# Latent attention's gate as seven block products a pair, with weight sums on GpSimd

## The reference

```
def _mla_layer(x, w_in, q_norm, w_uq, w_out, k_nope, k_rope, v):
    hproj = x @ w_in
    q_lat, gate = hproj[..., :Q_LORA], hproj[..., Q_LORA:]
    q = (_rms_norm(q_lat, q_norm) @ w_uq).reshape(b, s, H_B, QK_NOPE + QK_ROPE)
    ...
    o = _causal_block_attention(q_nope, q_rope, k_nope, k_rope, v).reshape(b, s, WIDTH_B)
    return (o * jax.nn.silu(gate)) @ w_out
```

## Time and profile before

| | |
|---|---|
| median of 3 runs | 1378.1 us (1377.26 to 1378.14) |
| profiled execution, its own time | 1378.76 us |
| span of the profile | 1376.7 us |
| PE busy | 1359.8 us, 99% |
| DVE busy | 1010.8 us, 73% |
| ACT busy | 745.6 us, 54% |
| POOL busy | 306.1 us, 22% |

### The profile page before, as it was taken

How to read it: one execution, slowest core, us unless ns; L and a number is a source line. 1 busy time by engine, 2 the same in 40 slices (tenths; PEclk the granted TensorE clock), 3 DMA queues, 4 the chain that set the end, 5 groups by cost and what they waited for, 6 DMA issues and landing times.

```text
span 1376.7 us, 19133 instructions
## 1 busy us (share of the span) xinstructions
PE 1359.8 (99%) x7308; PEld 1174.4 (85%) x7308; DVE 1010.8 (73%) x1671; ACT 745.6 (54%) x1197; POOL 306.1 (22%) x161
## 2 busy tenths in 40 slices
PE   8999999999999999999999999999999999999998
PEld 6788888888888888888888888878888999988887
DVE  7979787889933755454545479946877888889895
ACT  5453535457545534443444356658965666676554
POOL 2051414110043433433344210025304000000000
PEclk9999999999999999999999999999999999999999
DMA  7458575385367988966796558363122576455552
GB/s 269 164 180 225 194 206 186 127 281 206 134 186 216 312 216 238 296 171 167 212 300 161 153 212 305 123 202 124 67 85 77 162 206 169 149 181 214 196 190 103
DMA packets 53898, 260.37 MB, mean 189 GB/s; under 512 B 5568, under 2 KB 10304, under 8 KB 28224
## 3 DMA queue, kind: packets, MB, share of 16 engines
q1 hardware_dynamic: 37152, 163.04, 33.9%
q0 software_dynamic: 5760, 41.95, 15.5%
q10 hardware_dynamic: 10912, 54.40, 11.2%
HBM read 252.03 MB, written 91.23 MB: 249 GB/s over the span
## 4 chain that ended last, share of the span: by engine, by line
PE 82%; DVE 11%; DMA 2%; ACT 2%; issue 1%; POOL 1%; SPq 0%; DVEq 0%; ACTq 0%; POOLq 0%
PE bank L631 22%; PE bank L632 22%; PE bank L633 22%; PE bank L1362 6%; PE bank L1424 3%; PE bank L1313 3%; DVE wlo L2317 2%; PE bank L1341 1%; DMA stage<-in_w 1%; DMA v_spill<-v_tok 1%; DMA cols<-in_cols 1%; DVE wlo_a L2317 1%; DVE ar_lo L2317 1%; DVE xres L2495 1%; PE bank L1504 1%
## 5 line engine op out<-in xcount | busy, mean ns | idle before, releaser
L810 POOL TENSOR_TENSOR wlo<-stage,whi 128x1024 fp32r<-128x1024 f32 (+2 forms) x68 | 169.8, 2529 | 428.8 <-ACT whi L1644 342.5
L1647 ACT ACTIVATE whi<-stage 128x1024 fp32r<-128x1024 f32 (+2 forms) x155 | 148.2, 1002 | 104.2 <-PE bank L633 92.2
L2317 DVE TENSOR_TENSOR wlo<-stage,whi 128x1024 fp32r<-128x1024 f32 (+1 forms) x133 | 152.8, 1178 | 9.8 <-ACT whi L1647 9.8
L631 PE MATMUL bank<-xhi,whi 128*128 128x256 f32 (+1 forms) x300 | 98.4, 328 | 2.2 <-POOL wlo L946 1.2
L632 PE MATMUL bank<-xlo,whi 128*128 128x256 f32 (+1 forms) x300 | 98.1, 327 | 0.0
L633 PE MATMUL bank<-xhi,wlo 128*128 128x256 f32 (+1 forms) x300 | 98.0, 327 | 0.0
L1644 ACT ACTIVATE whi<-stage 128x1024 fp32r<-128x1024 f32 (+2 forms) x74 | 76.1, 1079 | 19.5 <-issue 14.3
L631 PE MATMUL bank<-whi,xhi 128*128 128x512 f32 (+1 forms) x204 | 78.3, 384 | 2.1 <-DVE wlo L2317 1.3
L633 PE MATMUL bank<-whi,xlo 128*128 128x512 f32 (+1 forms) x204 | 77.3, 379 | 0.0
L632 PE MATMUL bank<-wlo,xhi 128*128 128x512 f32 (+1 forms) x204 | 77.2, 378 | 0.0
L631 PEld LDWEIGHTS bank<-xhi,whi 128*128 128x128 f32 x300 | 57.0, 190 | 7.8 <-DVE hid L2527 1.4
(11 more groups left out here) (501 smaller groups left out, 4365.2 us busy)
## 6 DMA issues: line engine op xcount, KB each, us to landing
stage<-in_w SPq DMA_DIRECT2D x71, 1024.0 KB, 4.9
tsum<-in_w ACTq DMA_DIRECT2D x32, 1024.0 KB, 12.8
stage<-tsum SPq DMA_DIRECT2D x32, 1024.0 KB, 4.8
tsum<-in_w POOLq DMA_DIRECT2D x16, 1024.0 KB, 9.9
tsum<-tsum POOLq DMA_DIRECT2D x16, 1024.0 KB, 9.9
stage<-in_w SPq DMA_DIRECT2D x8, 1152.0 KB, 6.3
usum<-in_w POOLq DMA_DIRECT2D x8, 1024.0 KB, 10.0
stage<-usum SPq DMA_DIRECT2D x32, 256.0 KB, 4.1
```

The lines of the kernel that those rows point to most:

```text
L631: pe.matmul(dst, a_hi, b_hi, start=start, stop=False, skip_group_check=onto)
L810: pool.tensor_tensor(lo[:, to], stage[p % 2][:, r], hi[:, to].bitcast(F32), ALU.subtract).then_inc(w_lo, 1)
L1647: act.activation(dst, src, ACT.Copy, scale=scale).then_inc(signal, 1)
L2317: dve.tensor_tensor(dst, src, hi.bitcast(F32), ALU.subtract).then_inc(signal, 1)
```

## The change

The gate of a pair is a product of x (512 x 1024) with 1024 x 256 weights. It is cut into two by two blocks on either side, and is computed with seven block products (a scheme of Strassen and Winograd) where eight are plain. Each product is 12 matmuls of 256 columns (`gate_block`). The sums of x (`x_t1` to `x_t4`) are made once ahead of the loop: VectorE adds into `xsum`, ScalarE rounds, VectorE makes three remainders and GpSimd the fourth in the first pair. They lie in space of `vs_a`, `vs_b` (which is the first half of `xres`) and `xhi`, so `xres` is written out to `x_spill` ahead and read back behind the loop. The products are dealt over the pair: four between the scores of head 0 and its transposes, one after the scores of head 1, two after head 1's transposes.

The sums of the weights are made by GpSimd in the staging buffers (`gate_sum`, four of 512 columns a pair). The gate takes two panels, p+2 and p+3, so that a pair has four; of p+2 only 1536 columns are loaded and of p+3 1024, and 2048 and 1536 are split. Partial results are kept in `gate_kept` and summed by VectorE (`add_up`). The split of the next pair's query panel moves to the exponentials of head 1 (first half) and behind `tanh(0)` (second half). The copies for the last layer's sums are dealt over six pairs, one to three in each.

```
+            def gate_sum(pair, i):
+                p = M0 + 4 * pair + (3 if i == 4 else 2)
+                near, far = (stage[(M0 + k) % 2] for k in (0, 1))
+                to, x, y, op = ((slot(near, G_S1), slot(near, G_S3), slot(near, G_S1), ADD),
+                                (slot(near, G_S2), slot(near, G_S1), slot(near, G_A11), SUB),
+                                (slot(near, G_S3), slot(near, G_A11), slot(near, G_S3), SUB),
+                                (slot(far, G_S4), slot(far, G_A12), slot(near, G_S2), SUB))[i - 1]
+                if i in (1, 4):
+                    pool.wait_ge(landed[p % 2], LANDED[p % 2] + 16 * ((p - B0) // 2 + 1))
+                if i > 1:
+                    pool.wait_ge(m_ws, USED + 4 * pair + (2 if i == 4 else 1))
+                pool.tensor_tensor(to, x, y, op).then_inc(m_ws, 1)
...
+            for k in range(4 * PAIRS):
+                split_lo(M0 + k, PANEL if k % 4 == 0 else PAN)
...
+                if k == 0 or k > 1 and k % 4 == 1:
+                    for i in (1, 2, 3):
+                        gate_sum(k // 4, i)
...
                     scores(0)
-                    for i in range(24):
-                        gate_product(0, i)
+                    pe.wait_ge(t_l, USED + 3)
+                    pe.wait_ge(m_kvlo, c(4, 2))
+                    gate_block(x_t2, p + 2, G_S2, 0, bank[1][:, first_t])
+                    gate_block(x_t3, p + 2, G_S3, 0, bank[1][:, second_t]).then_inc(m_g, 1)
+                    gate_block(x_b11, p + 2, G_A11, 1, bank[0][:, first_t])
+                    gate_block(x_t1, p + 2, G_S1, 1, bank[0][:, second_t], True).then_inc(m_g, 1)
                     pe.wait_ge(m_kvlo, c(4, 4))
+                    pe.wait_ge(m_k, c(1, USED + 1))
                     for i in range(10):
                         turn(0, i)
                     scores(1)
-                    pe.wait_ge(m_gt, c(2, 3))
-                    for i in range(12):
-                        gate_product(1, i)
+                    pe.wait_ge(m_u, c(5, USED + 3))
+                    gate_block(x_b21, p + 3, G_A12, 0, bank[0][:, first_t], True)
                     attend(0, bank[1])
                     for i in range(10):
                         turn(1, i)
-                    for i in range(12, 24):
-                        gate_product(1, i)
+                    gate_block(x_b22, p + 3, G_S4, 0, bank[0][:, second_t], True).then_inc(m_g, 1)
+                    pe.wait_ge(t_l, USED + 4)
+                    gate_block(x_t4, p + 3, G_A22, 1, bank[5][:, first_t]).then_inc(m_g, 1)
                     attend(1, bank[7])
...
             act.wait_ge(n_x, TT)
+            act.dma_start(t["x_spill"], xres[:, 0:3, :]).then_inc(aux["x"], 16)
             act.dma_start(wkr[:, :], t["wkr"]).then_inc(aux["kr"], 16)
             act.dma_start(mask[:, :], t["mask"]).then_inc(aux["kr"], 16)
...
+            act.wait_ge(aux["x"], 32)
+            for i, x in enumerate((x_t3, x_t1, x_t2)):
+                act.wait_ge(t_s, USED + i + 1)
+                copy(x[0], xsum[:, (2, 0, 1)[i]], t_h)
...
                     exps(0)
+                    act.wait_ge(m_g, c(4, 5))
+                    act.wait_ge(m_gt, c(3, 3))
+                    copy(gate_kept[:, 0:SEQ], bank[1][:, :], m_k)
+                    act.wait_ge(m_ws, c(4, USED + 4))
+                    split_hi(p + 3, m_kv, c(4, 4), PAN, n)
...
                     exps(1)
+                    next_hi(0)
                     for b in range(3):
                         turned(1, b)
+                    act.wait_ge(m_u, c(5, USED + 4))
+                    tanh(0, first_t, bank[0][:, first_t])
+                    tanh(0, second_t, gate_kept[:, 0:HALF])
+                    next_hi(1)
                     if last and s == 1:
                         act.wait_ge(bld[0], 32)
                         operand_hi(BO, 0)
-                    tanh(1)
+                    act.wait_ge(m_u, c(5, USED + 5))
+                    tanh(1, slice(0, SEQ), gate_kept[:, HALF:])
...
+            s1, s2, s3, s4 = (xsum[:, i] for i in range(4))
+            own.mark(dve.tensor_tensor(s1, *plain(x_b12), ADD))
+            own.mark(dve.tensor_tensor(s2, *plain(x_b22), ADD))
+            own.settle()
+            dve.tensor_tensor(s3, s2, s1, SUB).then_inc(t_s, 1)
...
+            for i, x in enumerate((x_t3, x_t1, x_t2)):
+                dve.wait_ge(t_h, USED + i + 1)
+                lo_of(x[1], (s3, s1, s2)[i], x[0], t_l)
...
                     softmax(0)
+                    dve.wait_ge(m_k, c(1, USED + 1))
+                    dve.wait_ge(m_g, c(4, 6))
+                    add_up(0)
+                    dve.wait_ge(m_u, c(5, USED + 1))
+                    add_up(1)
+                    dve.wait_ge(m_u, c(5, USED + 2))
+                    add_up(2)
+                    for b in range(3):
+                        turned(0, b)
                     softmax(1)
                     for b in range(3):
                         turned(1, b)
+                    dve.wait_ge(m_g, c(4, 7))
+                    add_up(3)
+                    gates(0, 0, first_t, bank[0][:, first_t])
+                    gates(1, 0, second_t, kept[0])
+                    gated(0, bank[1])
+                    dve.wait_ge(m_g, c(4, 8))
+                    add_up(4)
                     if last and s == 1:
                         operand_lo(BO, 0)
-                    gates(1)
+                    gates(2, 1, slice(0, SEQ), gate_kept[:, HALF:])
                     gated(1, bank[7])
```

More of the change, by code:

```diff
@@ L710, in store @@
                                  gt[:, e, :]).then_inc(m_st[e], 16)
-            for j in range(6):
-                load(M0 + j, PANEL if j % 3 == 0 else PAN)
-            with sp.Fori(1, PAIRS // 2) as i:
-                for s in range(2):
[L716 to L720, removed]
+            load(M0, PANEL)
+            load(M0 + 1)
+            load(M0 + 2, PAN, 0, 512)
+            load(M0 + 3, 1024)
+            load(M0 + 4, PANEL)
+            load(M0 + 5)
+            load(M0 + 6, PAN, 0, 512)
+            with sp.Fori(0, PAIRS // 2 - 1) as i:
+                for s in range(2):
+                    store(2 * i + s)
+                    load(M0 + 4 * s + 7, 1024, 8 * i)
+                    load(M0 + 4 * s + 8, PANEL, 8 * i)
+                    load(M0 + 4 * s + 9, PAN, 8 * i)
+                    load(M0 + 4 * s + 10, PAN, 8 * i, 512)
+            store(PAIRS - 2)
+            load(L0 - 1, 1024)
             sp.wait_ge(w_lo, 2 * (L0 - 1))
             seven_load(BO, 0)
-            store(PAIRS - 2)
+            sp.wait_ge(m_g, 4 * PAIRS + 2)
+            sp.dma_start(xres[:, 0:2, :], t["x_spill"][:, 0:2, :]).then_inc(aux["x"], 16)
             sp.wait_ge(w_lo, 2 * L0)
@@ L1353, in attend, with gate_block @@
                         last.then_inc(m_o, 1)
-                    def gate_product(m, i):
-                        wh, wl = panel(p + 2, KX)
-                        k, f = i // 3, slice(m * P, (m + 1) * P)
-                        if m == 0 and i % 3 == 0:
-                            need(p + 2, n, KX, k)
-                        left, right = ((wh, xhi), (wh, xlo), (wl, xhi))[i % 3]
-                        last = pe.matmul(bank[0][:, :], left[:, k, f], right[:, k, :], start=i == 0, stop=i == 23)
-                        if i == 23:
-                            last.then_inc(m_g, 1)
+                    def gate_block(x, panel_, k, late, dst, onto=False):
+                        wh, wl = [slot(w[:, LINE:], k).rearrange("p (k n) -> p k n", k=PK) for w in parts(panel_)]
+                        pe.wait_ge(w_lo, 2 * n + (2 * panel_ + 1 + late))
+                        for kk in range(PK):
+                            last = split_dots(pe, dst, wh[:, kk, :], wl[:, kk, :], x[0][:, kk, :], x[1][:, kk, :],
+                                              kk == 0 and not onto, kk == PK - 1, onto)
+                        return last
                     pe.wait_ge(b_krlo, 4)
@@ L1636, in _, with split_hi @@
         def _(act):
-            def split_hi(p, used=None, count=0, width=PAN, n=0):
+            def split_hi(p, used=None, count=0, width=PAN, n=0, halves=(0, 1)):
                 act.wait_ge(landed[p % 2], 8 * n + LANDED[p % 2] + 16 * ((p - B0) // 2 + 1))
@@ L1641, in split_hi @@
                     act.wait_ge(used, count)
-                for s in range(2):
+                for s in halves:
                     r, to = half_at(p, s, width)
@@ L3003, in _ @@
             for d in range(2, 13):
+                if d == 8:
+                    dve.wait_ge(aux["x"], 64)
                 gathers(BO, 1, d)
```

151 lines of the change are left out of this document (101 added, 50 removed).

## The result

The changed kernel takes 1410.13 us (median of four runs, 1406.69 to 1418.57) beside 1378.12 of the kernel before on the same chip: ratio 1.0243, 95% interval 1.0197 to 1.0288, 32 us slower. Forecast were 1382 and a range of 1372 to 1390: right in sign, wrong in size. The profiled execution took 1409.27 (span 1407.5).

The account below looks back on a forecast made before the run. TensorE, busy 99% of the span, was taken as the bound, so removed matmul time is removed span. Terms: -8.4 + 4.0 + 2.1 + 0.5 + 2.0 + 0.5 + 3.0 = +3.7 us, forecast 1382, range 1372 to 1390.

Parts of the forecast that it names:

- the term of the sum DMAs: Pairs 2, 3, 6, 7: weight sums queue behind a DMA awaiting an accumulate; 0.5 us in all, bounds 0 and 8.
- rival (c): GpSimd's queue becomes the bound: accumulate landing past 12 us, scores wait 2 us in four pairs; 1390, chance 0.12.
- The gate's matmuls: Each pair's gate: 84 matmuls of 256 columns take 10.0 us against 11.05; gain 8.4 us in all.
- the estimate that the prediction made from the Trainium skill: Gate matmuls: straight line between page spacings gives 98 ns for 256 columns, a loss of 1.9 us a pair.
- Second transposes: Each pair: VectorE's two-SBUF-input sum waits for GpSimd, stalling the second transposes 0.5 us; 4.0 us in all.
- The next query panel: Pair's end: the next query panel's later split stalls TensorE 0.3 us, seven times; 2.1 us in all.
- Ahead of the loop: Before the pairs: x_spill delays loads, sums of x delay B0+4 (2.0 us); pair 0's weight sums hold a norm add (0.5).
- Behind the loop: First output product: operand rounding and remainder come later, TensorE stalls 3.0 us; bounds 1.5 and 3.5.
- rival (a): Whole kernel: the matmuls' gain survives, the loop stalls mostly go; -4 us, 1374, chance 0.21.

Follow-up runs that it names:

- e12: Changed kernel with its order of sum DMAs and weight sums kept, the sixteen copies issued ahead of the pair loop; 1397.75 us.
- m1: Test computing nothing of the reference: eight GpSimd sum DMAs of 1 MB, 512 bytes of descriptor scratch; each issue waited for the landing ahead (10.64, 20.51).
- e5: Changed kernel with the weight sums first and every sum DMA moved, none behind the query panel at a pair's start; 1383.66 us, ratio 1.0043.
- e2: Changed kernel with the three weight sums ahead of the sum DMA that follows split_lo(p+1), nothing else moved; 1396.6 us.
- e8: e6 with the first output product's operand rounded and its remainder taken ahead of the last pair's gate sums and tanh; 1376.15 us.
- e6: e5 with the first output product's eight weight copies dealt over pairs 0 and 1, the other sixteen over pairs 2 to 6; 1373.06 us, ratio 0.9965.
- m2: The same eight sum DMAs as m1 with 2048 bytes of descriptor scratch; seven went out at once, the eighth at the seventh landing (44.27).

## Why the prediction was wrong

- **The step that failed** is the term of the sum DMAs, 0.5 us with bounds 0 and 8, and the price and pairs of rival (c), 1390 at a chance of 0.12. The mechanism was told link by link as it came: accumulate, weight sums, ScalarE, `kn_hi`, scores. Even its threshold, "free up to a landing time of 12 us", stands between the 10.5 of e12 (free) and the 14.6 of pair 3 (1.6 us). Three sizes in it were wrong. The landing was taken from a median, 9.9; beside two or three copies, the stores and the loads of a pair's start it was 14.5 to 16.3, and the single transfers of the old timeline (issued at 544.56, landed at 562.08, beside copies too) would have said so. The pairs were taken to be those where a semaphore asks for the earlier sums; GpSimd stood before a sum DMA in every pair from 1 on, which is what m1 shows for a ring of 512 bytes. And in pair 1 a second sum DMA, ahead of the `split_lo(p+1)` itself, was overlooked: 8.97 us of wait. e5, which has e2's order too, puts 26 us of the 32 on the places of these DMAs and the weight sums, the slow matmuls behind the waits included.
- **The clock** was no term at all. The four waits above add up to 29 us; loop and gains would need some 42 (32.4 of loss and about 10 of gain). The transposes take 2 of the rest and the query product 1. Some 9 are matmuls at the lower clock behind five of the waits: in pair 1 the keys' product takes 8.23 us for 5.44, and in pairs 0, 2, 4 and 5 one scores block takes 4.54 to 4.62 for some 3.0.
- **The gate's matmuls**, -8.4: right way, too small, and past its bound of 9.3. Seven blocks take 9.65 us a pair in e5_respread (12 matmuls in 1.36 to 1.38, 0.114 each) where 10.0 was forecast: 1.4 gained a pair, -11.2 in all. The V product, the nearest row, still takes its 0.1177 each in the changed kernels; the gate's spacing is another. With the longer query product (0.07) and second transposes (0.26) taken off, such a pair is 46.21 - 45.15 = 1.06 shorter. The rows also stay apart from the estimate that the prediction made from the Trainium skill, "TensorE: Matmul & The Clock Gate", section Back-to-back issue gap: there 256 columns cost three quarters of 512 (98 and 131 ns), here half (114 and 227).
- **Second transposes**, 4.0: mechanism right (the sum took 1.12 where 1.0 was forecast, R to the second transposes 7.30), size 0.27 a pair, 2.2 in all. It shows as longer transposes, not as a listed wait.
- **The next query panel**, 2.1: no wait on `wlo` in pairs 2 to 7; the query product takes 12.35 to 12.47 for 12.30, at most 1.
- **Ahead of the loop**, 2.0 + 0.5: +0.65. `wkr` did queue behind the store (it landed 6.2 us after its issue, 2.2 before), `wkr_hi` came at 399.75 (401 forecast), `c_hi` at 415.74 (417.5), and B0+4 was complete at 425.6 (427.2) with no wait of TensorE: the chain was 1.6 to 1.8 us shorter than I had added up.
- **Behind the loop**, 3.0: 2.6, the best of the terms. What e8 adds is that it was also a cover for two others.
- **Pair 0**, no term: 6 us. The eight copies at 441 were there before, but now more hangs on the loads beside them. A load issued at 453.83 landed at 470.30, the fourth weight sum began at 470.42, and it and the splits behind it held VectorE's softmax until 481.1 (rows below), for which TensorE waited 3.5 us. That dealing out these copies mends the pair is shown by e6.

With these sizes and without the sum DMAs my sum would have been -11.2 + 2.2 + 1 + 0.65 + 2.6 = -4.8, which is rival (a); e6, at -5, is that kernel. The chance given to it, 0.21, was not the mistake; the 0.12 for (c), with a price of 8, was. That the forecast had the right sign is luck: its plus came from terms that measured less than forecast, and the loss from the one put at 0.5.

## What to carry to other kernels

An instruction that issues a DMA is a wait if the queue's ring is full: when work is moved behind one, price it by the landings at that very place, the worst and not the median, and ask how many may be in flight. A kernel whose TensorE never waits has no slack measured anywhere; a wait of some 3 us can also take the clock, so count it higher than its length (29 us of waits came with some 9 of slow matmuls here). And when a wait is removed at a stage's end, look what it was covering before counting it as a gain.

## What the runs showed of the hardware

- A sum DMA of 1 MB on GpSimd's queue: with 512 bytes of scratch one was in flight (m1), with 2048 seven (m2); the eighth then went out behind the landing of the seventh (44.27), not of the first (9.60). The seven were issued 0.52 us apart.
- GpSimd's work also held a VectorE operation with a single tensor input, where that and the output lie in SBUF; the prediction counted only those with two. Pair 0 of the changed kernel, where its fourth weight sum came late; in the other pairs these three take 0.29, 0.42 and 0.35:

```profile
472.11 2.20 DVE L3068 TENSOR_SCALAR prob<-prob,sm 128x128 f32<-128x128 f32 x1
474.41 2.38 DVE L3068 TENSOR_SCALAR prob<-prob,sm 128x384 f32<-128x384 f32 x1
476.89 4.17 DVE L3068 TENSOR_SCALAR prob<-prob,sm 128x256 f32<-128x256 f32 x1
```

  GpSimd ran from 470.42 to 480.9, with one DMA issue in between (476.51). The Trainium skill, "GPSIMD Engine Reference", section Specifications, names two kinds of contenders for the shared interface, VectorE instructions with two SBUF inputs and those in a 2-port mode; the rows agree if this operation is of the second kind, which no run here shows by itself.

- The clock behind a wait is not certain. 2.64 us on `br_lo` was followed by a first product of 12.37 us in e5_respread, and of 11.01 in the changed kernel. The first 4 us of each, e5_respread first (clock 0.57 and 1.00):

```profile
812.00:816.00 4.00, 3.37 (x9) 2.71 (x10) 3.90 (x5) 1.36 (x2) 0.00 (x0) 0.57 1.04 431
844.00:848.00 4.00, 3.30 (x14) 2.74 (x15) 3.90 (x5) 1.41 (x2) 0.00 (x0) 1.00 1.05 431
```
